# Attention's value products of a head for all 512 queries at once, with two heads of turned probabilities kept, in a three-part block kernel on Trainium2

## The chip, the cores and the metric

The kernel runs on one core of a Trainium2 chip. The metric is the device time of one execution in microseconds (us), here the median over several executions. TensorE (PE, with its weight loads shown apart as PEld), VectorE (DVE), ScalarE (ACT) and GpSimd (POOL) each run their own instruction stream in order and meet at semaphores. SyncE (SP) issues most of the transfers.

## The reference

A sequence of 512 tokens of width 1024 passes two layers of one kind (three mixers side by side and a mixture of experts) and then one layer of another kind with a dense feed-forward. The change touches the first two layers. There, an input projection gives, among others, a query part of rank 256 and a key/value part of rank 128 per token; both are normalised and multiplied by weights into 8 heads of queries, keys and values. What attention computes for a head is:

```python
s = (jnp.einsum('bqhd,bkhd->bhqk', qn_b, k_nope)
     + jnp.einsum('bqhr,bkr->bhqk', qr_b, k_rope)).astype(F32) * scale
p = jax.nn.softmax(s, axis=-1).astype(v.dtype)
return jnp.einsum('bhqk,bkhd->bqhd', p, v)
```

Two scans (an mLSTM and an SSD, each in both directions) follow from the same projection. Then comes the product with `w_out`, a layer norm and the experts.

## The kernel before

The program is a row of stages with a barrier of all engines between them. In each of the first two layers these are, among others, `in_projection`, `mla` (attention), `scans`, `norm_stage` (product with `w_out` and layer norm), a router and the experts. Numbers are kept at full precision by splitting a factor into a high and a low part (type fp32r): a product is three matmuls, `TERMS = ((0, 0), (0, 1), (1, 0))`. The high part is a cast by ACT, the low part a subtraction by DVE or POOL.

`mla` works in 32 tiles, i = 4h + t for the 8 heads h and the 4 blocks t of 128 queries, as a software pipeline written out by hand. The order of every engine's instructions is that of its loop over steps. In step s, PE (L555 to L570) does:

- `scores_of(s)` (L528): 3 matmuls of 512 columns into one of four banks, which must be free of the tile four before.
- `turned(s-3)` (L536): 4 transposes of the normalised probabilities into bank 4 or 5. It waits for the tile to be normalised and for the low part of tile s-5.
- `values_of(u, ks)` (L551) from step 6 on: for half a head u (256 queries) and two of the four key blocks, 6 matmuls of 256 columns with 64 columns of weights, into `O` (bank 6). A half head takes two steps. Its first step waits for the low parts of its two tiles; the first half of a head also waits for `head_home`, the copy of the previous head out of `O`.
- at t = 0 `query(h+1)` (L507), at t = 1 `key(h+1)` (L512), for h up to 6; in head 0 also `value(t)` (L517).

ACT in step s does: the copy of turned tile s-4 into `PT` as its high part (L595); at t = 2 from step 10 on, the copy of the finished head out of `O` (L599); at t = 1 the high part of the next query (L579), at t = 2 that of the next key (L585); the exponential of tile s (L609); and at t = 3 of heads 1 to 4 a cast of 512 columns for the scans (`KQ`, L616). DVE in step s does: the row maximum of tile s (L640), the reciprocal of the row sum of tile s-1 (L646), the low part of tile s-4 into `PT` (L653), the home copy of the next query at t = 0 (L626), the low part of the next key at t = 2 (L632). POOL normalises the tiles (L686) and makes the low part of the next query (L677).

`PT` is a ring of three half heads. `CQ` holds the normalised query and key/value inputs (three planes of 512 columns); it is written by `in_projection` in place (L429, L432) and read by `mla`. `raw` is a ring of four 1 MB weight chunks: `in_projection` reads its ten chunks of `w_in` through it, chunk i in slot i % 4, and `w_low` counts the chunks that POOL (L470) has finished with. In `mla`, slots 2 and 3 hold attention's weights, and SP loads the first two chunks of `w_out` into slots 0 and 1 (L498); `norm_stage` takes them (ACT, L1073, after `out_in` has reached 32). In `scans` SP issues 16 loads of gate rows `ROW` into a ring of 6 (L725); from s = 6 on each waits for the decay of stream s-6.

Of the kernel before, what the change touches and what calls it, by code (L numbers as in the profile page):

```python
# [21 lines left out]
F32 = mybir.dt.float32  # L22
F32R = mybir.dt.float32r
I32 = mybir.dt.int32
ALU = mybir.AluOpType
# [3 lines left out]
P = 128  # L29
S = 512  # L30
NT = S // P
# [14 lines left out]
C_QN, C_KVN, C_CW, C_CB, C_DS, C_SN, C_SGN, C_SB, C_AL, C_IB, C_MN, C_LG, C_LB, C_L2G, C_L2B, C_N = 0, 2, 3, 33, 39, 41, 43, 44, 45, 46, 47, 49, 57, 65, 73, 81  # L46
# [7 lines left out]
TERMS = ((0, 0), (0, 1), (1, 0))  # L54
# [157 lines left out]
def in_projection(nc, m, layer, mx, a, XS, WS):  # L212
# [11 lines left out]
    with stage(nc, "in_projection", *names) as (block, sems):  # L224
# [21 lines left out]
        def _(pe):  # L246
# [38 lines left out]
            for t in range(NT):  # L285
                if t == 2:
                    pe.wait_ge(m.mla_in, 16)
                    pe.wait_ge(home, K0 - 7)
                    pe.wait_ge(home, KV2 + 1)
                    pe.matmul(m.ps[K0 % 8][0:64, :], m.w_mla[:, 2048:2112], mx.CQ[:, 2, :], start=True, stop=True).then_inc(unit_done, 1)  # L290
                    pe.wait_ge(home, Q0 - 7)
                    pe.wait_ge(home, Q2 + 1)
                    for k in range(2):
                        last = pe.matmul(m.ps[Q0 % 8][:, :], m.w_mla[:, k * 1024:k * 1024 + P], mx.CQ[:, k, :], start=(k == 0), stop=(k == 1))
                    last.then_inc(unit_done, 1)
                pe.wait_ge(home, V[t] - 7)
                step = 0
                for k in range(KD):
                    for hw, hx in TERMS:
                        last = pe.matmul(m.ps[V[t] % 8][:, 0:256], XS[:, hx, k, t * P:(t + 1) * P], WS[:, i % 2, hw, k * 256:(k + 1) * 256],  # L300
                                         start=(step == 0), stop=(step == 3 * KD - 1))
                        step += 1
                last.then_inc(unit_done, 1)
# [59 lines left out]
        def _(dve):  # L363
# [62 lines left out]
            bank = home_of(GT)  # L426
            dve.tensor_copy(mx.GN[:, :, :, :].rearrange("p a t r -> p (a t r)"), bank[:, 0:2 * NT * GR]).then_inc(home, 1)
            dve.wait_ge(inv_rms, 1)
            dve.scalar_tensor_tensor(out=mx.CQ[:, 2, :], in0=mx.CQ[:, 2, :], scalar=m.CP[:, C_KVN:C_KVN + 1], in1=RS[0], op0=ALU.mult, op1=ALU.mult).then_inc(home, 1)  # L429
            dve.wait_ge(inv_rms, 2)  # L430
            for c in range(2):
                last = dve.scalar_tensor_tensor(out=mx.CQ[:, c, :], in0=mx.CQ[:, c, :], scalar=m.CP[:, C_QN + c:C_QN + c + 1],  # L432
                                                in1=RS[1], op0=ALU.mult, op1=ALU.mult)
            last.then_inc(home, 1)
            dve.wait_ge(kr_high, 1)
# [40 lines left out]
def mla(nc, m, layer, mx, a):  # L476
# [5 lines left out]
    with stage(nc, "mla", *names) as (block, sems):  # L482
# [10 lines left out]
        @block.sync  # L493
        def _(sp):
            sp.dma_start(m.gate_dram, mx.NM[0:GR, :]).then_inc(rows_out, 16)
            sp.wait_ge(rows_out, 16)
            for q in range(2):
                sp.dma_start(m.raw[:, q, :], m.d["w_out"][bass.ds(layer, 1), q].rearrange("a p n -> p (a n)")).then_inc(m.out_in, 16)  # L498

        @block.tensor  # L500
        def _(pe):

            def query(h):
                if h >= 2:
                    pe.wait_ge(k_low, h - 1)
                for k in range(2):
                    last = pe.matmul(Q[:, :], wq[:, k, h * P:(h + 1) * P], mx.CQ[:, k, :], start=(k == 0), stop=(k == 1))  # L507
                last.then_inc(q_done, 1)

            def key(h):  # L510
                pe.wait_ge(q_home, h)
                pe.matmul(Q[0:64, :], wk[:, h * 64:(h + 1) * 64], mx.CQ[:, 2, :], start=True, stop=True).then_inc(k_done, 1)  # L512

            def value(t):
                if t >= 1:
                    pe.wait_ge(v_low, t)
                pe.matmul(O[:, :], mx.CQ[:, 2, t * P:(t + 1) * P], wv, start=True, stop=True).then_inc(v_done, 1)  # L517

            def scores_of(i):
                h, t = divmod(i, NT)  # L520
# [15 lines left out]
                    last = pe.transpose(m.ps[4 + i % 2][:, k * P:(k + 1) * P], PR[:, i % 4, k * P:(k + 1) * P], m.ident[:, :])  # L536
                last.then_inc(probs_t, 1)

            def values_of(u, ks):

                h, half = divmod(u, 2)
                if ks[0] == 0:
                    pe.wait_ge(pt_low, 2 * u + 2)
                    if u == 0:
                        pe.wait_ge(v_low, NT)
                    if half == 0 and h >= 1:
                        pe.wait_ge(head_home, h)
                n = 0
                for k in ks:
                    for hv, hp in TERMS:  # L550
                        last = pe.matmul(O[0:64, half * 256:(half + 1) * 256], a.VS[:, hv, k, h * 64:(h + 1) * 64], a.PT[:, u % 3, hp, k, :],  # L551
                                         start=(k == 0 and n == 0), stop=(k == NT - 1 and n == 3 * len(ks) - 1))
                        n += 1
                last.then_inc(pv, 1)

            for step in range(NI + 6):
                h, t = divmod(step, NT)
                if step < NI:
                    scores_of(step)
                if 3 <= step < NI + 3:  # L560
                    turned(step - 3)
                if step >= 6:
                    u, part = divmod(step - 6, 2)
                    values_of(u, (2 * part, 2 * part + 1))
                if step < NI:
                    if t == 0 and h + 1 < HEADS:
                        query(h + 1)
                    if t == 1 and h + 1 < HEADS:
                        key(h + 1)
                    if h == 0:  # L570
                        value(t)

        @block.scalar
        def _(act):
# [9 lines left out]
                    act.wait_ge(scores, NT * (h - 1))  # L584
                act.copy(a.KS[h % 2][0:64, 0, :], Q[0:64, :]).then_inc(k_high, 1)  # L585

            for step in range(NI + 7):
                h, t = divmod(step, NT)
                if 4 <= step < NI + 4:
                    i = step - 4  # L590
                    act.wait_ge(probs_t, i + 1)
                    u = i // 2
                    if u >= 3:
                        act.wait_ge(pv, 2 * (u - 2))
                    act.copy(a.PT[:, u % 3, 0, :, i % 2 * P:(i % 2 + 1) * P], m.ps[4 + i % 2][:, :].rearrange("p (k n) -> p k n", k=NT)).then_inc(pt_high, 1)  # L595
                if step >= 10 and t == 2:
                    hp = (step - 10) // NT
                    act.wait_ge(pv, 4 * (hp + 1))
                    act.copy(m.XT[64 * (hp % 2):64 * (hp % 2) + 64, hp // 2, :], O[0:64, :]).then_inc(head_home, 1)  # L599
                if step < NI:  # L600
                    if h + 1 < HEADS:
# [18 lines left out]
        def _(dve):  # L620
# [13 lines left out]
            for step in range(NI + 4):  # L634
# [11 lines left out]
                    dve.reciprocal(a.RC[:, i % 4:i % 4 + 1], a.SM[:, i % 4:i % 4 + 1]).then_inc(inv_sum, 1)  # L646
                if step >= 4:
                    i = step - 4
                    u = i // 2
                    dve.wait_ge(pt_high, i + 1)  # L650
                    if u >= 3:
                        dve.wait_ge(pv, 2 * (u - 2))
                    dve.tensor_tensor(a.PT[:, u % 3, 1, :, i % 2 * P:(i % 2 + 1) * P], m.ps[4 + i % 2][:, :].rearrange("p (k n) -> p k n", k=NT),  # L653
                                      a.PT[:, u % 3, 0, :, i % 2 * P:(i % 2 + 1) * P].bitcast(F32), ALU.subtract).then_inc(pt_low, 1)
                if step < NI:
                    if h + 1 < HEADS:
                        if t == 0:
# [28 lines left out]
                pool.tensor_scalar(PR[:, i % 4, :], PR[:, i % 4, :], a.RC[:, i % 4:i % 4 + 1], None, ALU.mult).then_inc(probs_normed, 1)  # L686


def scans(nc, m, mx, g):

# [16 lines left out]
    with stage(nc, "scans", *names) as (block, sems):  # L709
# [10 lines left out]
        @block.sync  # L720
        def _(sp):
            for s in range(NS):
                if s >= RR:
                    sp.wait_ge(decay, 4 * (s - RR + 1))
                sp.dma_start(g.ROW[:, s % RR, :], m.gate_dram[row_of[s]:row_of[s] + 1, :].to_broadcast([P, S])).then_inc(row_in[s % RR], 16)  # L725

        @block.gpsimd
        def _(pool):
# [1916 lines left out]
def sb(nc, ctx, name, *shape):  # L2645

    return ctx.enter_context(nc.sbuf_tensor(f"{name}_{nc.next_id()}", list(shape), F32))


def sbr(nc, ctx, name, *shape):  # L2650

    return ctx.enter_context(nc.sbuf_tensor(f"{name}_{nc.next_id()}", list(shape), F32R))
# [7 lines left out]
def build(nc, d, out):  # L2660
    with ExitStack() as ctx:
# [24 lines left out]
        with ExitStack() as c1:  # L2686
# [14 lines left out]
            for layer in range(DEPTH):  # L2701
# [15 lines left out]
                with ExitStack() as c2:  # L2717
# [11 lines left out]
                    mx.GN = sb(nc, c2, "GN", P, 2, NT, GR)  # L2729
                    mx.XN = sb(nc, c2, "XN", P, NT, 256)  # L2730
                    with ExitStack() as c3:
                        mx.CQ = sb(nc, c3, "CQ", P, 3, S)
                        mx.KRT = sb(nc, c3, "KRT", P, S)
                        mx.TP = m.XT[:, 7, :]
                        a = Bag()
                        a.QS = [sbr(nc, c3, "QS", P, 2, S)]
                        a.KS = [sbr(nc, c3, "KS", P, 2, S)]
                        with ExitStack() as c4:
                            WS = sbr(nc, c4, "WS", P, 2, 2, KD * 256)
                            if layer == 0:  # L2740
                                transpose_stage(nc, m, XS0, first_loads, layer_params)
                            in_projection(nc, m, layer, mx, a, XS0, WS)
# [4 lines left out]
                        a.QS.append(sbr(nc, c3, "QS", P, 2, S))  # L2747
                        a.KS.append(sbr(nc, c3, "KS", P, 2, S))
                        a.VS = sbr(nc, c3, "VS", P, 2, NT, S)
                        a.PT = sbr(nc, c3, "PT", P, 3, 2, NT, 256)  # L2750
                        a.NM = sb(nc, c3, "NM", P, 4)
                        a.SM = sb(nc, c3, "SM", P, 4)
                        a.RC = sb(nc, c3, "RC", P, 4)
# [1 line left out]
                    with ExitStack() as c3:  # L2755
# [11 lines left out]
                        g.YI = c3.enter_context(nc.sbuf_tensor(f"YI_{nc.next_id()}", [P, 2, S], F32, side="right"))  # L2767
                        g.DEN = sb(nc, c3, "DEN", P, S)
                        g.RD = sb(nc, c3, "RD", P, S)
                        scans(nc, m, mx, g)  # L2770
                with ExitStack() as c2:
                    ln = Bag()
                    ln.GB = sb(nc, c2, "GB", P, 2 * D)
# [310 lines left out]
```

## Time and profile before

| | |
|---|---|
| median of three runs | 1982.55 us (1981.88 to 1986.97) |
| profiled execution, first to last instruction | 1984.4 us |
| mean granted TensorE clock over the span | 0.928 of full speed |
| PE busy over the span | 86% |
| `mla` of layer 0 | from 153.4 us to 241.5 us |
| `mla` of layer 1 | from 765.6 us to 853.8 us |

The page of the profile gives the span of the profiled execution; no other time of that same execution is listed. The busy shares of the whole span are means over stages with different limits, so what the change is worth has to be read from the two `mla` stages, which together take 176 of the 1984 us.

### The profile page before, as it was taken

Reading aid. Unit: us, or ns where it says so; the run is one execution under the profiler, and the core shown is the slowest. Engines: PE = TensorE matmul, PEld = TensorE weight load, DVE = VectorE, ACT = ScalarE, POOL = GpSimd, SP = SyncE. Lnnn points to the kernel's source line nnn. Section 1 sums busy time; section 2 is a strip of 40 time slices with the busy share of each in tenths; the row PEclk is TensorE's granted clock in tenths of the full one; section 3 lists DMA queues with packets and bytes.
Section 4 is the critical chain, followed back from the end, with each engine's and each line's share of the span. In section 5 each row is a group of like instructions: output and inputs, shape, how many; then the busy total and the mean of one; then the engine's idle time right before and its main releaser. Section 6 shows DMA issues by size and latency. Waiting matters only on the chain. (4 is left out here: it accounts for less than half of the span.)

```text
span 1984.4 us, 22134 instructions
## 1 busy us (share of the span) xinstructions
PE 1707.1 (86%) x8018; PEld 1330.5 (67%) x8018; DVE 1153.0 (58%) x1721; ACT 901.3 (45%) x1371; POOL 634.5 (32%) x337
## 2 busy tenths in 40 slices
PE   5999997849982999988949992699896689999998
PEld 4876743748871876752737872587686578888887
DVE  3936565559975745746858985487455424233242
ACT  3246576238875235756327883435443331111112
POOL 2336632112211434731201210153622124444442
PEclk9999998969995999989969996799898899999999
DMA  4201011069954211020257983320000223222221
GB/s 186 85 32 45 30 57 64 12 275 346 374 216 187 97 54 45 1 70 16 85 210 305 365 324 131 132 97 31 21 1 1 85 109 115 90 101 102 90 85 43
DMA packets 40480, 233.93 MB, mean 118 GB/s; under 512 B 9316, under 2 KB 9700, under 8 KB 20660
## 3 DMA queue, kind: packets, MB, share of 16 engines
q1 hardware_dynamic: 31012, 215.46, 28.6%
q0 software_dynamic: 9216, 16.80, 2.3%
q8 instruction: 65, 1.06, 0.2%
q14 instruction: 43, 0.35, 0.1%
q10 hardware_dynamic: 144, 0.26, 0.1%
HBM read 226.03 MB, written 23.23 MB: 126 GB/s over the span
## 5 line engine op out<-in xcount | busy, mean ns | idle before, releaser
L259 PE MATMUL bank<-XS,WS 128*128 128x512 f32 x864 | 207.4, 403 | 15.8 <-DVE WS L384 15.8
L2561 POOL TENSOR_TENSOR WS<-ring,WS 128x2048 fp32r<-128x2048 f32 x31 | 149.3, 4817 | 188.2 <-ACT WS L2543 188.2
L259 PEld LDWEIGHTS bank<-XS,WS 128*128 128x128 f32 x864 | 166.0, 192 | 56.9 <-DVE WS L384 16.4
L1382 PE MATMUL bank<-WS,XS 128*128 128x512 f32 x768 | 189.1, 403 | 1.1 <-DVE XS L1502 1.1
L2543 ACT CAST WS<-ring 128x2048 fp32r<-128x2048 f32 x31 | 59.3, 1913 | 271.4 <-PE bank L2578 143.8
L2578 PE MATMUL bank<-XS,WS 128*128 128x512 f32 x768 | 174.9, 389 | 2.7 <-DVEq L2616 2.7
L2596 PE MATMUL bank<-WS,US 128*128 128x512 f32 x768 | 174.7, 389 | 0.0
L1382 PEld LDWEIGHTS bank<-WS,XS 128*128 128x128 f32 x768 | 146.1, 194 | 32.2 <-DVE XS L1502 1.9
L2578 PEld LDWEIGHTS bank<-XS,WS 128*128 128x128 f32 x768 | 144.1, 188 | 32.7 <-POOLq L2557 2.9
L2596 PEld LDWEIGHTS bank<-WS,US 128*128 128x128 f32 x768 | 144.2, 188 | 29.9
L1846 PE MATMUL bank<-XS,WS 128*128 128x512 f32 x576 | 135.6, 396 | 3.6 <-POOLq L2035 2.6
L1846 PEld LDWEIGHTS bank<-XS,WS 128*128 128x128 f32 x576 | 109.1, 190 | 28.7 <-POOLq L2035 2.8
L470 POOL TENSOR_TENSOR WS<-raw,WS 128x2048 fp32r<-128x2048 f32 x18 | 83.9, 4659 | 114.5 <-ACT WS L314 114.5
L686 POOL TENSOR_SCALAR XT<-XT,RC 128x512 f32<-128x512 f32 x64 | 100.2, 1567 | 45.0 <-DVE RC L646 44.8
L1345 POOL DMA_INDIRECT mixed_rows<-YE,table x32 | 33.5, 1047 | 248.4 <-DVE table L1519 147.2
L2633 DVE TENSOR_TENSOR X<-X,bank 128x512 f32<-128x512 f32 x32 | 22.0, 688 | 141.6 <-PE bank L2596 141.6
L1406 PE MATMUL bank<-DS,HT 128*128 128x512 f32 x384 | 98.1, 405 | 6.2 <-DVE DS L1509 6.1
L1496 DVE TENSOR_TENSOR WS<-raw,WS 128x2048 fp32r<-128x2048 f32 x32 | 73.1, 2289 | 27.1 <-ACT WS L1443 27.1
L1406 PEld LDWEIGHTS bank<-DS,HT 128*128 128x128 f32 x384 | 72.4, 194 | 21.2 <-issue 6.5
L1006 PE MATMUL bank<-WS,XS 128*128 128x512 f32 x360 | 83.5, 392 | 0.0
L314 ACT CAST WS<-raw 128x2048 fp32r<-128x2048 f32 x18 | 34.3, 1906 | 103.5 <-PE bank L259 103.5
L2038 POOL TENSOR_TENSOR WS<-ring,WS 128x2048 fp32r<-128x2048 f32 x11 | 53.5, 4864 | 79.5 <-ACT WS L1868 79.5
(531 smaller groups left out, 3486.4 us busy)
## 6 DMA issues: line engine op xcount, KB each, us to landing
raw<-in_w_exp SPq DMA_DIRECT2D x16, 2048.0 KB, 14.8
DN<-in_w_exp SPq DMA_DIRECT2D x32, 1024.0 KB, 10.5
ring<-in_w_ff SPq DMA_DIRECT2D x32, 1024.0 KB, 4.8
raw<-in_w_in SPq DMA_DIRECT2D x20, 1024.0 KB, 4.8
GU<-in_w_exp SPq DMA_DIRECT2D x8, 2048.0 KB, 17.1
XT<-in_w_exp SPq DMA_DIRECT2D x8, 2048.0 KB, 17.5
ring<-in_w_in SPq DMA_DIRECT2D x12, 1024.0 KB, 5.1
raw<-in_w_out SPq DMA_DIRECT2D x8, 1024.0 KB, 4.8
```

The lines of the kernel that those rows point to most:

```text
L259: last = pe.matmul(m.ps[g % 8][:, :], WS[:, i % 2, hw, at:at + P], XS[:, hx, k, :], start=(step == 0), stop=(step == 3 * KD - 1))
L470: pool.tensor_tensor(WS[:, i % 2, 1, :], m.raw[:, i % 4, :], WS[:, i % 2, 0, :].bitcast(F32), ALU.subtract).then_inc(w_low, 1)
L686: pool.tensor_scalar(PR[:, i % 4, :], PR[:, i % 4, :], a.RC[:, i % 4:i % 4 + 1], None, ALU.mult).then_inc(probs_normed, 1)
L1006: last = pe.matmul(m.ps[2 * t + half][:, :], XS[:, hx, 4 * kh + k, t * P:(t + 1) * P], WS[:, 2 * kh + half, hw, k * S:(k + 1) * S], start= ...
L1382: last = pe.matmul(m.ps[2 + e % 2][:, :], r.XS[:, e % 2, hx, 4 * half + k, :], r.WS[:, half, hw, k * S:(k + 1) * S], start=(half == 0 and ...
L1406: last = pe.matmul(m.ps[5 + half][:, :], r.HT[:, hx, f * P:(f + 1) * P], r.DS[:, hw, at:at + S], start=(n == 0), stop=(n == 5))
L1496: dve.tensor_tensor(r.WS[:, half, 1, :], r.GU[e % 4][:, half * 4 * S:(half + 1) * 4 * S], r.WS[:, half, 0, :].bitcast(F32), ALU.subtract). ...
L1846: last = pe.matmul(bank[u][:, :], q.WS[:, i % 2, hw, at:at + P], b.XS[:, hx, k, :], start=(step == 0), stop=(step == 3 * KD - 1))
L2543: act.copy(f.WS[:, q % 2, 0, :], f.ring[:, q % 4, :]).then_inc(w_high, 1)
L2561: pool.tensor_tensor(f.WS[:, q % 2, 1, :], f.ring[:, q % 4, :], f.WS[:, q % 2, 0, :].bitcast(F32), ALU.subtract).then_inc(w_low, 1)
L2578: last = pe.matmul(m.ps[mine + u % 4][:, :], f.WS[:, q % 2, hw, k * 256 + c * P:k * 256 + (c + 1) * P], f.XS[:, hx, k, :], start=(n == 0), ...
L2596: last = pe.matmul(bank[:, :], f.US[:, hx, 4 * kh + k, t * P:(t + 1) * P], f.WS[:, q % 2, hw, k * S:(k + 1) * S], start=(kh == 0 and n == ...
```

## The change

The value products of a head are made in four steps of three matmuls, each over all 512 queries and one block of keys, in place of two halves with two steps of six matmuls over 256 queries. They start at step 8 in place of step 6, and the loop has two steps more. `PT` keeps two whole heads in place of three half heads. The copy of a finished head by ACT moves from t = 2 (from step 10) to t = 0 (from step 12). To make room, the normalised inputs move from `CQ` into slot 0 of `raw` under the name `CN`, so `in_projection` waits for `w_low` at 9 before it writes them; `CQ` and `KRT` are freed after `in_projection`. The two loads of `w_out` move from `mla` into `scans`, behind the row loads s = 7 and s = 9.

```diff
@@ in_projection
             dve.wait_ge(inv_rms, 1)
+            dve.wait_ge(w_low, NB - 1)
-            dve.scalar_tensor_tensor(out=mx.CQ[:, 2, :], in0=mx.CQ[:, 2, :], scalar=m.CP[:, C_KVN:C_KVN + 1], in1=RS[0], op0=ALU.mult, op1=ALU.mult).then_inc(home, 1)
+            dve.scalar_tensor_tensor(out=mx.CN[:, 2, :], in0=mx.CQ[:, 2, :], scalar=m.CP[:, C_KVN:C_KVN + 1], in1=RS[0], op0=ALU.mult, op1=ALU.mult).then_inc(home, 1)
...
@@ mla, SP
             sp.wait_ge(rows_out, 16)
-            for q in range(2):
-                sp.dma_start(m.raw[:, q, :], m.d["w_out"][bass.ds(layer, 1), q].rearrange("a p n -> p (a n)")).then_inc(m.out_in, 16)
@@ mla, PE
-            def values_of(u, ks):
-
-                h, half = divmod(u, 2)
-                if ks[0] == 0:
-                    pe.wait_ge(pt_low, 2 * u + 2)
-                    if u == 0:
+            def values_of(h, k):
+
+                if k == 0:
+                    pe.wait_ge(pt_low, NT * (h + 1))
+                    if h == 0:
                         pe.wait_ge(v_low, NT)
-                    if half == 0 and h >= 1:
+                    if h:
                         pe.wait_ge(head_home, h)
-                n = 0
-                for k in ks:
-                    for hv, hp in TERMS:
-                        last = pe.matmul(O[0:64, half * 256:(half + 1) * 256], a.VS[:, hv, k, h * 64:(h + 1) * 64], a.PT[:, u % 3, hp, k, :],
-                                         start=(k == 0 and n == 0), stop=(k == NT - 1 and n == 3 * len(ks) - 1))
-                        n += 1
+                for n, (hv, hp) in enumerate(TERMS):
+                    last = pe.matmul(O[0:64, :], a.VS[:, hv, k, h * 64:(h + 1) * 64], a.PT[:, h % 2, hp, k, :],
+                                     start=(k == 0 and n == 0), stop=(k == NT - 1 and n == 2))
                 last.then_inc(pv, 1)
 
-            for step in range(NI + 6):
+            for step in range(NI + 8):
...
-                if step >= 6:
-                    u, part = divmod(step - 6, 2)
-                    values_of(u, (2 * part, 2 * part + 1))
+                if step >= 8:
+                    values_of(*divmod(step - 8, NT))
@@ mla, ACT
-            for step in range(NI + 7):
+            for step in range(NI + 9):
...
-                    u = i // 2
-                    if u >= 3:
-                        act.wait_ge(pv, 2 * (u - 2))
-                    act.copy(a.PT[:, u % 3, 0, :, i % 2 * P:(i % 2 + 1) * P], m.ps[4 + i % 2][:, :].rearrange("p (k n) -> p k n", k=NT)).then_inc(pt_high, 1)
-                if step >= 10 and t == 2:
-                    hp = (step - 10) // NT
-                    act.wait_ge(pv, 4 * (hp + 1))
+                    hi, ti = divmod(i, NT)
+                    if hi >= 2:
+                        act.wait_ge(pv, NT * (hi - 1))
+                    act.copy(a.PT[:, hi % 2, 0, :, ti * P:(ti + 1) * P], m.ps[4 + i % 2][:, :].rearrange("p (k n) -> p k n", k=NT)).then_inc(pt_high, 1)
+                if step >= 12 and t == 0:
+                    hp = (step - 12) // NT
+                    act.wait_ge(pv, NT * (hp + 1))
                     act.copy(m.XT[64 * (hp % 2):64 * (hp % 2) + 64, hp // 2, :], O[0:64, :]).then_inc(head_home, 1)
@@ mla, DVE: the same ring of two heads and the same wait for pv in the low part
...
@@ scans, SP
                 sp.dma_start(g.ROW[:, s % RR, :], m.gate_dram[row_of[s]:row_of[s] + 1, :].to_broadcast([P, S])).then_inc(row_in[s % RR], 16)
+                if s in (RR + 1, RR + 3):
+                    q = (s - RR) // 2
+                    sp.dma_start(m.raw[:, q, :], m.d["w_out"][bass.ds(layer, 1), q].rearrange("a p n -> p (a n)")).then_inc(m.out_in, 16)
@@ build
-                        mx.CQ = sb(nc, c3, "CQ", P, 3, S)
-                        mx.KRT = sb(nc, c3, "KRT", P, S)
+                        mx.CN = m.raw[:, 0, 0:3 * S].rearrange("p (c n) -> p c n", c=3)
...
-                        a.PT = sbr(nc, c3, "PT", P, 3, 2, NT, 256)
+                        a.PT = sbr(nc, c3, "PT", P, 2, 2, NT, S)
```

## Rows read from the trace of the kernel before

**Rows 1.** Windows: the two mla stages, busy us per engine, clock, DMA.
```profile
153.30:241.50 88.20, 84.28 (x466) 61.17 (x466) 57.60 (x118) 58.00 (x127) 59.82 (x40) 1.00 0.07 26
765.50:853.70 88.20, 84.29 (x466) 61.20 (x466) 57.61 (x118) 58.02 (x127) 59.83 (x40) 1.00 0.07 26
```

**Rows 2.** Waits in mla of layer 0: us in total, times, longest.
```profile
PE bank L551 <- ACT XT L599: 0.5, 1, 0.5
```

**Rows 3.** Timeline around 193 us: weight loads of one step at t = 3.
```profile
192.10 0.54 PEld L528 LDWEIGHTS bank<-KS,QS 128*128 128x128 f32 x3
...
192.74 0.54 PEld L536 LDWEIGHTS bank<-ident,XT 128*128 128x128 f32 x4
...
193.25 0.71 PEld L551 LDWEIGHTS bank<-PT,VS 128*64 128x64 f32 x6
...
193.94 0.53 PEld L528 LDWEIGHTS bank<-KS,QS 128*128 128x128 f32 x3
```

**Rows 4.** Timeline 222 to 256 us: heads 6 and 7 and the tail.
```profile
225.33 0.57 ACT L595 CAST PT<-bank 128x512 fp32r<-128x512 f32 x1
...
225.88 0.71 PEld L551 LDWEIGHTS bank<-PT,VS 128*64 128x64 f32 x6
...
228.99 0.58 ACT L595 CAST PT<-bank 128x512 fp32r<-128x512 f32 x1
...
229.59 0.58 ACT L599 COPY XT<-bank 64x512 f32<-64x512 f32 x1
...
230.28 0.67 PEld L551 LDWEIGHTS bank<-PT,VS 128*64 128x64 f32 x6 [0.70 <-issue]
...
230.93 0.55 PEld L528 LDWEIGHTS bank<-KS,QS 128*128 128x128 f32 x3
...
233.35 0.57 ACT L595 CAST PT<-bank 128x512 fp32r<-128x512 f32 x1
...
235.97 0.42 PEld L536 LDWEIGHTS bank<-ident,XT 128*128 128x128 f32 x4
...
236.85 2.83 PEld L551 LDWEIGHTS bank<-PT,VS 128*64 128x64 f32 x24 [0.46 <-DVE PT L653]
...
237.28 0.69 DVE L653 TENSOR_TENSOR PT<-bank,PT 128x512 fp32r<-128x512 f32 x1 [0.51 <-ACT PT L595]
239.98 0.58 ACT L599 COPY XT<-bank 64x512 f32<-64x512 f32 x1 [2.73 <-PE bank L551]
```

**Rows 5.** Timeline 168 to 190 us: step 12, behind a KQ cast.
```profile
184.26 0.61 ACT L616 CAST KQ<-MQ 128x512 fp32r<-128x512 f32 x1
...
184.77 0.58 ACT L595 CAST PT<-bank 128x512 fp32r<-128x512 f32 x1
184.82 0.71 PEld L551 LDWEIGHTS bank<-PT,VS 128*64 128x64 f32 x6
```

**Rows 6.** The same timeline: scores at t = 2 of head 1 and 2.
```profile
169.73 0.53 PEld L528 LDWEIGHTS bank<-KS,QS 128*128 128x128 f32 x3 [0.81 <-issue]
...
180.01 0.53 PEld L528 LDWEIGHTS bank<-KS,QS 128*128 128x128 f32 x3 [0.81 <-ACT XT L609]
```

**Rows 7.** The same timeline: step 8, low part of tile 3, turn of tile 5.
```profile
173.27 0.66 DVE L653 TENSOR_TENSOR PT<-bank,PT 128x512 fp32r<-128x512 f32 x1
...
174.05 0.53 PEld L536 LDWEIGHTS bank<-ident,XT 128*128 128x128 f32 x4
```

**Rows 8.** DMA issues 150 to 300 us: KB each, median us to landing.
```profile
raw<-in_w_out SPq DMA_DIRECT2D x2, 1024.0 KB, 5.8
```

**Rows 9.** Timelines of SP and ACT: row load s = 7, first use of w_out.
```profile
254.81 0.32 SPq L725 DMA_DIRECT2D ROW<-gate_rows  x1
...
330.75 1.05 ACT L1073 CAST WS<-raw 128x1024 fp32r<-128x1024 f32 x1 [1.92 <-PEq L77]
```

**Rows 10.** Timeline 130 to 430 us: end of the input projection.
```profile
138.30 0.75 DVE L429 SCALAR_TENSOR_TENSOR CQ<-CQ,CP,XT 128x512 f32<-128x512 f32 x1 [5.14 <-ACT XT L350]
...
147.55 1.31 POOL L472 TENSOR_TENSOR QS<-XT,QS 128x512 fp32r<-128x512 f32 x1 [20.09 <-ACT QS L359]
```

More of the change, by code:

```diff
@@ L289, in _ @@
                     pe.wait_ge(home, KV2 + 1)
-                    pe.matmul(m.ps[K0 % 8][0:64, :], m.w_mla[:, 2048:2112], mx.CQ[:, 2, :], start=True, stop=True).then_inc(unit_done, 1)
+                    pe.matmul(m.ps[K0 % 8][0:64, :], m.w_mla[:, 2048:2112], mx.CN[:, 2, :], start=True, stop=True).then_inc(unit_done, 1)
                     pe.wait_ge(home, Q0 - 7)
@@ L293, in _ @@
                     for k in range(2):
-                        last = pe.matmul(m.ps[Q0 % 8][:, :], m.w_mla[:, k * 1024:k * 1024 + P], mx.CQ[:, k, :], start=(k == 0), stop=(k == 1))
+                        last = pe.matmul(m.ps[Q0 % 8][:, :], m.w_mla[:, k * 1024:k * 1024 + P], mx.CN[:, k, :], start=(k == 0), stop=(k == 1))
                     last.then_inc(unit_done, 1)
@@ L428, in _ @@
             dve.wait_ge(inv_rms, 1)
-            dve.scalar_tensor_tensor(out=mx.CQ[:, 2, :], in0=mx.CQ[:, 2, :], scalar=m.CP[:, C_KVN:C_KVN + 1], in1=RS[0], op0=ALU.mult, op1=ALU.mult).then_inc(home, 1)
+            dve.wait_ge(w_low, NB - 1)
+            dve.scalar_tensor_tensor(out=mx.CN[:, 2, :], in0=mx.CQ[:, 2, :], scalar=m.CP[:, C_KVN:C_KVN + 1], in1=RS[0], op0=ALU.mult, op1=ALU.mult).then_inc(home, 1)
             dve.wait_ge(inv_rms, 2)
             for c in range(2):
-                last = dve.scalar_tensor_tensor(out=mx.CQ[:, c, :], in0=mx.CQ[:, c, :], scalar=m.CP[:, C_QN + c:C_QN + c + 1],
+                last = dve.scalar_tensor_tensor(out=mx.CN[:, c, :], in0=mx.CQ[:, c, :], scalar=m.CP[:, C_QN + c:C_QN + c + 1],
                                                 in1=RS[1], op0=ALU.mult, op1=ALU.mult)
@@ L506, in query @@
                 for k in range(2):
-                    last = pe.matmul(Q[:, :], wq[:, k, h * P:(h + 1) * P], mx.CQ[:, k, :], start=(k == 0), stop=(k == 1))
+                    last = pe.matmul(Q[:, :], wq[:, k, h * P:(h + 1) * P], mx.CN[:, k, :], start=(k == 0), stop=(k == 1))
                 last.then_inc(q_done, 1)
@@ L511, in key @@
                 pe.wait_ge(q_home, h)
-                pe.matmul(Q[0:64, :], wk[:, h * 64:(h + 1) * 64], mx.CQ[:, 2, :], start=True, stop=True).then_inc(k_done, 1)
+                pe.matmul(Q[0:64, :], wk[:, h * 64:(h + 1) * 64], mx.CN[:, 2, :], start=True, stop=True).then_inc(k_done, 1)
             def value(t):
@@ L516, in value @@
                     pe.wait_ge(v_low, t)
-                pe.matmul(O[:, :], mx.CQ[:, 2, t * P:(t + 1) * P], wv, start=True, stop=True).then_inc(v_done, 1)
+                pe.matmul(O[:, :], mx.CN[:, 2, t * P:(t + 1) * P], wv, start=True, stop=True).then_inc(v_done, 1)
             def scores_of(i):
@@ L648, in _ @@
                     i = step - 4
-                    u = i // 2
+                    hi, ti = divmod(i, NT)
                     dve.wait_ge(pt_high, i + 1)
[L651 to L654, printed above, removed]
+                    if hi >= 2:
+                        dve.wait_ge(pv, NT * (hi - 1))
+                    dve.tensor_tensor(a.PT[:, hi % 2, 1, :, ti * P:(ti + 1) * P], m.ps[4 + i % 2][:, :].rearrange("p (k n) -> p k n", k=NT),
+                                      a.PT[:, hi % 2, 0, :, ti * P:(ti + 1) * P].bitcast(F32), ALU.subtract).then_inc(pt_low, 1)
                 if step < NI:
@@ L686, in _, with scans @@
                 pool.tensor_scalar(PR[:, i % 4, :], PR[:, i % 4, :], a.RC[:, i % 4:i % 4 + 1], None, ALU.mult).then_inc(probs_normed, 1)
-def scans(nc, m, mx, g):
+def scans(nc, m, layer, mx, g):
     streams = [("mlstm", h, d, h) for h in range(4) for d in range(2)]
@@ L2738, in build @@
                         with ExitStack() as c4:
+                            mx.CQ = sb(nc, c4, "CQ", P, 3, S)
+                            mx.KRT = sb(nc, c4, "KRT", P, S)
                             WS = sbr(nc, c4, "WS", P, 2, 2, KD * 256)
@@ L2769, in build @@
                         g.RD = sb(nc, c3, "RD", P, S)
-                        scans(nc, m, mx, g)
+                        scans(nc, m, layer, mx, g)
                 with ExitStack() as c2:
```

## The prediction

> **What bounds the kernel now.** I read the windows of the two `mla` stages first. Each lasts 88.2 us, PE is busy for 84.3 of them at a granted clock of 1.00 (2.4 GHz), no other engine for more than 60, and both layers are alike to 0.02 us [rows 1]. So each term below is worked out in layer 0 and taken twice. Then the timeline. In a step without query or key, PE's weight loads stand back to back: scores start at 192.10, the turn at 192.74, the value products at 193.25, the next scores at 193.94 [rows 3]. That is 0.64 + 0.51 + 0.69 = 1.84 us with no gap: PE sets the pace, and the other engines run one to three steps beside it.
>
> The waits of PE on the copy of a finished head were the third view. Of eight such copies in a layer just one kept PE waiting [rows 2]. It is the one of step 30, in head 7, where no key product stands between the last products of a head and the first of the next. There ACT's order decides. It copies turned tile 26 at 228.99, then the head at 229.59, and the products start at 230.28 [rows 4]. Two steps earlier, with no copy due, the tile copy starts at 225.33 and the products at 225.88 [rows 4]. The products thus start 1.29 after the tile copy in place of 0.55: the copy of a head costs PE 0.74 us where nothing covers it. At t = 2 of the other heads PE has about 1 us of key products ahead of that place, and they cover it.
>
> **The change part by part.**
>
> *Half as many value products, twice as wide.* 192 of 256 columns become 96 of 512 in each layer; the columns streamed are the same. Six narrow ones take 0.69 us; three of 512 columns, by the scores in the same rows, 0.64 [rows 3]. The gain is 0.05 us a step; its lower bound is nothing (the same columns), its upper bound this 0.05, since no row shows a 512-column product in a shorter slot. I take 0.05. From step 8 to step 31 it counts in 24 steps, but in the five where PE then waits for ACT (next part) it only lengthens the wait: 19 x 0.05 = 0.95 us a layer.
>
> The Trainium skill, "TensorE: Matmul & The Clock Gate", section "Back-to-back issue gap", gives N/2.4 + 2.5 ns a product, an estimate of 6 x 109.2 against 3 x 215.8 ns, so a gain of 0.008 us a step. The trace shows six times that. By the page's rule the sum below would be 1.6 us higher, 12.8 in place of 11.2.
>
> *The head copy moves from t = 2 to t = 0.* Now the last products of a head close step t = 3, which has neither query nor key, and the next head's products come after only scores and turn, as in step 30. ACT can't be earlier: after the exponential of the step before, it first copies the turned tile. Queued behind PE's wait stand the query, the next scores, and with them every engine. Steps 12, 16, 20, 24 and 28 have it. In 24 and 28 it costs the 0.74 worked out above. In 12, 16 and 20 ACT's `KQ` cast (0.61) comes ahead of the tile copy too: there the tile copy starts at 184.77 and the products at 184.82 [rows 5]. With 1.29 after the tile copy they start at 186.06, a wait of 1.24. Sum: 3 x 1.24 + 2 x 0.74 = 5.20 us. The wait of step 30 goes: -0.74. Lower bound of this part nothing, if PE has hidden slack to make it up (rival 2); upper bound 5.20. I take 4.46 net, since PE shows no slack.
>
> *Steps 6 and 7 lose their products.* That is 2 x 0.69 = 1.38 us less for PE early on. But step 8 can't start its turn before the low part of tile 3, which ends at 173.27 + 0.66 = 173.93; PE turns at 174.05 today [rows 7]. What is late next is thus DVE's chain. I take nothing; the upper bound is 1.38 us a layer.
>
> *The tail.* I count from T, the start of the last scores (230.93 now). Today the last turn is at T + 5.04, the last half head's low part ends at T + 7.04, and ACT takes the last head at T + 9.05 [rows 4]. In the new order ACT copies tile 28 at T + 2.42 as now, and head 5 behind it, so the products of step 32 start at T + 3.71 and take 0.64. The turn of tile 30 and its products follow until T + 5.49. The turn of tile 31 (0.51) and the last two product steps of head 6 end at T + 7.27. Now the copy of head 6 stands alone between two heads. ACT started 0.32 us after the end of 24 product slots of 0.117 [rows 4], so it copies at T + 7.59, and PE resumes 0.69 later at T + 8.28. Low part 31, about two us behind its turn as now, is earlier. All 12 products of head 7 follow: 12 x 0.213 = 2.56. ACT takes the last head at T + 11.16, 2.1 us later than now. Lower bound: just the 2.56 against today's 1.38 of the last half, 1.2 us.
>
> *The rest I cost at nothing.* The new wait for `w_low` in `in_projection`: POOL had been idle for 20 us at 147.55, so it was done by 127.5, and DVE gets there at 138.3 [rows 10]. Without that cover DVE would stand still until POOL has finished chunk 8. Writing to `raw` in place of `CQ` keeps sizes and instructions. The ring of two heads makes ACT and DVE wait at step 4h + 4 for products that closed the step before. The head copy waits for the same event, so this is already counted. The two `w_out` loads stand on SP's queue behind the row load s = 7 (254.81) and two further on. 1 MB lands in 5.8 us, and `norm_stage` first reads it at 330.75 [rows 8, 9]: some 60 us of cover. A row load behind one is late by 5.8 us at most, and it is issued six streams ahead in a stage whose streams take over 4 us each. In `mla` nothing queued behind these loads.
>
> **Sum.** Per layer 4.46 - 0.95 + 2.1 = 5.6 us, for both 11.2. The profiled span is 1984.4; what lies around it is not shown, and the median of the runs, 1982.55, is 1.85 below the span, so I add the difference to the median: 1993.8 us, slower by 0.57%. I count changes within 0.3% (6 us) as no change: about what a measurement of this kernel can tell.
>
> **Rivals.**
> 1. *The start is kept.* If step 8 is not held by DVE, the 1.38 us a layer are a gain: 1993.8 - 2.8 = 1991.0. Rows 7 speak against it, by 0.12 us.
> 2. *The other side: the copy is paid for where it left.* At t = 2 the scores of head 2 start after 0.81 us that the profile puts down to ACT [rows 6], and ACT no longer copies a head in that step. If this idle time is ACT's, each of five heads gets back up to 0.81: 4.05 a layer, and 1993.8 - 8.1 = 1985.7, no change. It decides if the 0.81 falls below about 0.3. Against it: head 1, with no copy due, has the same 0.81 [rows 6], so it looks like the drain behind the key product.
> 3. *A row load is late.* If `w_out` holds up a row that the scans need, 5.8 us twice a layer at most: up to 2017. The six-stream lead speaks against it.
> 4. *The change brings what its count says.* If narrow products cost PE more than their slots show and the three wide ones free more than 0.05, the gain must exceed 5.6 us in 24 steps of a layer, 0.23 a step, to break even. The slot of 0.213 for a wide product leaves no room.
>
> **Chances.** Forecast 0.62 (its own range 1990 to 1998), rival 1 0.15, rival 2 0.13, rival 3 0.03, rival 4 0.04, the rest 0.03. With forecast, 1 and 3, less a few hundredths for spread between runs, slower is 0.80. Rival 2 and that spread make no change 0.16, and faster is 0.04. Range: the bounds together give per layer, at the low end, 4.46 - 1.2 + 1.2 - 1.38 = 3.1, which is 1988.7, and at the high end 4.46 + 2.1 = 6.6, which is 1995.7. Down to 1986 takes in most of rival 2. Runs of before differ by 5 us, so the top is 1998.
>
> **What would show it.** 96 value matmuls a layer, in threes, with 0.64 to the next scores. At steps 12, 16 and 20 PE waits some 1.2 us for L599's copy at its new line, at 24 and 28 some 0.7, at 30 not at all. `mla` takes about 93.8 us in place of 88.2, and its last head copy comes 11 us after the last scores. The turn of step 8 starts as now. The scans take the same time, with no wait for a row. Wrong would be: `mla` no longer than 90 us, the 0.81 at t = 2 gone, or a difference of over 2 us outside the two stages.

## The result and the profile after

The changed kernel takes 1992.15 us in the median of five runs (1987.21 to 1995.61), the kernel before 1981.88 in five (1980.48 to 1986.97): a ratio of 1.005 with a 95% interval of 1.0033 to 1.0066. That is 10.3 us slower; forecast were 11.2 us, as 1993.8 us in a range of 1986 to 1998.

The windows of the two attention stages after answer to [rows 1] (columns as there: length, busy us of PE, PEld, DVE, ACT and POOL, clock, DMA share, GB/s):

```profile
152.50:246.50 94.00, 85.02 (x370) 52.02 (x370) 57.64 (x118) 58.01 (x127) 59.72 (x40) 1.00 0.01 2
...
766.80:860.90 94.10, 85.10 (x370) 52.03 (x370) 57.63 (x118) 57.99 (x127) 59.72 (x40) 1.00 0.01 2
```

Each stage has 96 matmuls fewer (370 for 466) and is longer by 5.9 us (94.06 and 94.10 from its first transfer to the scans' first, for 88.16 and 88.17). The two make 11.8 us, more than the whole difference of the medians. PE is busy 0.8 us longer in a stage 5.9 us longer: it waits. The view of waits in the stage of layer 0 says for whom (left of the arrow who waited, right of it for whom; us in total, times, longest). Before, PE's waits for the head copy were one of 0.5 [rows 2]:

```profile
ACT XT L593 <- PE bank L547: 3.9, 2, 3.1
PEld bank L547 <- issue: 3.6, 4, 1.1
PE bank L547 <- ACT XT L593: 3.5, 5, 0.9
```

L547 are the value products, L593 is ACT's copy of a finished head. Of the five hand-overs the view puts four to the copy and that of step 16 to a low part by DVE that ends at the same moment; the products of that step need low parts that were done 1.9 us before, so there too it is the copy. Step 12 in the timeline answers to [rows 5], step 24 to the stretch of [rows 4] that showed the one wait of before:

```profile
183.23 0.61 ACT L610 CAST KQ<-MQ 128x512 fp32r<-128x512 f32 x1
...
183.74 0.58 ACT L589 CAST PT<-bank 128x512 fp32r<-128x512 f32 x1
184.22 0.58 ACT L593 COPY XT<-bank 64x512 f32<-64x512 f32 x1
...
184.91 0.42 PEld L547 LDWEIGHTS bank<-PT,VS 128*64 128x64 f32 x3 [1.13 <-issue]
184.94 0.87 PE L547 MATMUL bank<-PT,VS 128*64 128x512 f32 x3 [0.92 <-ACT XT L593]
```
```profile
217.31 0.58 ACT L589 CAST PT<-bank 128x512 fp32r<-128x512 f32 x1
...
217.91 0.58 ACT L593 COPY XT<-bank 64x512 f32<-64x512 f32 x1
...
218.60 0.42 PEld L547 LDWEIGHTS bank<-PT,VS 128*64 128x64 f32 x3 [0.73 <-issue]
```

Cast, tile copy, head copy follow one another on ACT without a gap, and PE's weight loads stand still for 1.13 us where the cast is ahead and 0.73 where it isn't. The tail of layer 0, from the last scores on, is the third place:

```profile
233.57 0.65 PEld L527 LDWEIGHTS bank<-KS,QS 128*128 128x128 f32 x3
...
241.27 0.58 ACT L593 COPY XT<-bank 64x512 f32<-64x512 f32 x1 [0.80 <-PE bank L547]
...
241.96 2.49 PEld L547 LDWEIGHTS bank<-PT,VS 128*64 128x64 f32 x12 [1.22 <-DVE PT L647]
241.99 2.95 PE L547 MATMUL bank<-PT,VS 128*64 128x512 f32 x12 [0.76 <-ACT XT L593]
244.97 0.58 ACT L593 COPY XT<-bank 64x512 f32<-64x512 f32 x1 [3.13 <-PE bank L547]
```

The last head copy starts 11.40 us after the last scores (244.97 - 233.57), against 9.05 before [rows 4]. All 12 products of head 7 stand behind the copy of head 6.

The profiled execution of after has a span of just 1985.5 us, 1.1 more than that of before, though its attention stages alone are 11.8 us longer. It is the fastest of its five runs (1987.21). The stage of router and experts, which the change doesn't touch, takes 202.7 and 204.2 us in it, and 206.1 twice in the profile of before; over all profiles of this study it lies between 202.3 and 206.1. In this pair of profiles the two make up half of the 10.7 us by which all that lies outside attention is shorter; the other half is spread over the other stages. Attention stages agree between their two layers to 0.1 us. So below the stage's length decides, and the medians follow it only roughly.

### The profile page after: what moved, and what is told of

It is laid out like the page before. It is cut to its first block and busy times, and to the rows that moved or that the text cites. A ratio compares the mean times of both kernels' runs of the same rounds, so it can differ in the third digit from the quotient of the medians.

```text
span 1985.5 us, 21746 instructions
## 1 busy us (share of the span) xinstructions
PE 1701.4 (86%) x7826; PEld 1308.6 (66%) x7826; DVE 1150.5 (58%) x1721; ACT 899.9 (45%) x1371; POOL 634.1 (32%) x337
```

## The experiments

The starts of the scores in the weight-load timeline give the length of each PE step. The table has the steps that differ (us, layer 0; step 10 stands for all steps at t = 2 from there on, which agree to 0.03; the stage runs from its first transfer to the first one of the scans, "last scores at" counts from its start, and "rest" is what follows the start of the last scores):

| | before | after | e1 two out banks | e2 copy first | e3 narrow | e5 cast moved | e7 before, two banks |
|---|---|---|---|---|---|---|---|
| step 6 | 1.83 | 1.14 | 1.13 | 1.13 | 1.14 | 1.13 | 1.83 |
| step 8 | 3.25 | 3.79 | 3.80 | 3.80 | 3.81 | 3.80 | 3.24 |
| step 10 | 1.83 | 1.71 | 1.69 | 1.72 | 1.83 | 1.69 | 1.83 |
| step 12 | 3.23 | 4.44 | 3.34 | 3.95 | 4.32 | 3.91 | 3.24 |
| step 16 | 3.24 | 4.57 | 3.33 | 4.06 | 4.43 | 4.06 | 3.24 |
| step 20 | 3.23 | 4.44 | 3.35 | 3.95 | 4.32 | 3.91 | 3.24 |
| step 24 | 3.23 | 4.05 | 3.35 | 3.58 | 3.91 | 4.03 | 3.23 |
| step 28 | 1.84 | 2.39 | 1.82 | 1.93 | 2.37 | 2.40 | 1.84 |
| step 30 | 2.52 | 1.83 | 1.83 | 1.83 | 1.84 | 1.82 | 1.84 |
| last scores at | 77.54 | 81.08 | 76.50 | 78.71 | 81.34 | 79.57 | 76.88 |
| rest | 10.62 | 12.98 | 11.79 | 13.18 | 12.93 | 13.02 | 10.29 |
| stage | 88.16 | 94.06 | 88.29 | 91.89 | 94.27 | 92.59 | 87.17 |

**e1: the wait taken away.** The products of even and odd heads go to two banks (bank 3 comes from the scores, which keep three), so a head's products wait only for the copy of the head before the last. Theory: the wait for the copy and the tail are the loss. Rival: the longer pipeline, the moved inputs or the late loads are, and the waits only show it.

```diff
+        OB = (m.ps[6], m.ps[3])
...
-                    if h:
-                        pe.wait_ge(head_home, h)
+                    if h >= 2:
+                        pe.wait_ge(head_home, h - 1)
...
-                    last = pe.matmul(O[0:64, :], a.VS
+                    last = pe.matmul(OB[h % 2][0:64, :], a.VS
...
-                    last = pe.matmul(m.ps[i % 4][:, :], a.QS
+                    last = pe.matmul(m.ps[i % 3][:, :], a.QS
```

> The changed kernel with the products of even and odd heads in two banks, so that a head's products wait for the copy of the head before the last (the scores get three banks in place of four). Theory (the wait of PE for ACT's copy of a head, plus the longer tail, is the loss): all five waits at steps 12 to 28 and the two in the tail go; per layer 24 x 0.05 = 1.2 us and the 0.74 of step 30 are gained against the kernel before, and a tail of about 0.9 us is lost, so the attention stage takes about 87.1 us (94.1 changed, 88.2 before) and the kernel about 1980 us. Rival (the longer pipeline, the moved inputs or the late loads cost the time, the waits only show it): the stage stays above 92 us.

1981.06 us, against 1981.44 for the kernel before, measured beside it: a ratio of 0.9998 (0.9988 to 1.0007). The stage takes 88.29 us. At step 12 the products now start while the tile copy is still running, and ACT takes the finished head later, with nobody waiting:

```profile
184.90 0.59 ACT L590 CAST PT<-bank 128x512 fp32r<-128x512 f32 x1
184.92 0.47 PEld L548 LDWEIGHTS bank<-PT,VS 128*64 128x64 f32 x3
...
185.37 0.58 ACT L594 COPY XT<-bank 64x512 f32<-64x512 f32 x1
```

This kernel has every other part of the change: the wide products, the two-head ring, the inputs in `raw`, the late loads. The theory holds, and the rival falls. But the stage was expected at 87.1, and the 1.2 us that are missing have to be found (they are added up under "Sum" below).

**e2: the order on ACT.** The head copy (the block with L593) stands ahead of the tile copy in the same step; nothing else differs.

```diff
+                if step >= 12 and t == 0:
+                    ... head copy
                 if 4 <= step < NI + 4:
                     ... tile copy
-                if step >= 12 and t == 0:
-                    ... head copy
```

> The changed kernel with ACT's copy of a finished head ahead of the copy of the turned tile in the same step. Theory (PE waits because the copy stands behind the tile copy in ACT's order): each of five waits gets shorter by the 0.58 us of a tile copy, so about 2.8 us per layer, the stage takes about 91.3 us in place of 94.1, the kernel about 1986.5. Rival (PE waits for the latency between the products' end and the copy, not for the order): the stage stays at 94.

1991.2 us, ratio 1.005 (1.0033 to 1.0067); by the median no better than after, by the stage 2.2 us a layer (91.89 and 91.94). The five steps shrink by 0.49, 0.51, 0.49, 0.47 and 0.46 us; the tail grows by 0.2, since the low parts there now come behind. Order is the cause, but a tile copy costs the queue about 0.48 us, not 0.58. ACT begins the next instruction that early (183.74 to 184.22 in step 12 above).

**e5: the cast.** The KQ cast moves from t = 3 of heads 1 to 4 to t = 0 of the next head, behind the exponential.

```diff
-                    if t == 3 and 1 <= h <= 4:
-                        c, kq = divmod(h - 1, 2)
+                    if t == 0 and 2 <= h <= 5:
+                        c, kq = divmod(h - 2, 2)
```

> The changed kernel with ACT's KQ cast moved from t = 3 of heads 1 to 4 to t = 0 of the next head, behind the exponential, so that it no longer stands ahead of the head copy. Theory: steps 12, 16 and 20 fall from 4.44, 4.57 and 4.44 us to the 4.05 of step 24, where no cast stands ahead: 1.3 us per layer, stage 92.8 us, kernel about 1989.5. Rival (PE catches the cast up elsewhere, or waits for latency alone): stage 94.1.

1988.15 us, ratio 1.0035 (1.0022 to 1.0048), stage 92.59 and 92.63. Steps 12, 16 and 20 fall to 3.91, 4.06 and 3.91, that is to about step 24's length (4.03), and steps 24 and 28 stay: the cast is on PE's path in three heads of a layer.

**e3: narrow products in the new order.** Each wide product is two of 256 columns again.

```diff
-                for n, (hv, hp) in enumerate(TERMS):
-                    last = pe.matmul(O[0:64, :], ... a.PT[:, h % 2, hp, k, :],
+                for half in range(2):
+                    at = slice(half * 256, (half + 1) * 256)
+                    for n, (hv, hp) in enumerate(TERMS):
+                        last = pe.matmul(O[0:64, at], ... a.PT[:, h % 2, hp, k, at],
```

> The changed kernel with the order kept, but each value product again as two of 256 columns, six in a step. Theory: a step costs 0.05 us more, in the 19 steps without a wait, and the last 12 products become 24 (0.25 us): 1.2 us more per layer, stage 95.3 us, kernel about 1994.5. Rival by the rule of 2.5 ns per product: 0.008 a step, stage 94.3.

1992.78 us, ratio 1.0057 (1.0041 to 1.0074); the stage takes 94.27 and 94.26, 0.2 us more than with wide products. The 0.05 us a step of the theory is too high by some four times. Half as many matmuls over the same columns save PE next to nothing here.

**e4: the loads alone.** The kernel before with the two loads of `w_out` in the scans.

```diff
-            for q in range(2):
-                sp.dma_start(m.raw[:, q, :], ...).then_inc(m.out_in, 16)
...
+                if s in (RR + 1, RR + 3):
+                    q = (s - RR) // 2
+                    sp.dma_start(m.raw[:, q, :], ...).then_inc(m.out_in, 16)
```

> The kernel before with just the two loads of w_out moved into the scans. Theory: hidden, no change (1982 us within 2; the scans stage 89.2 us as before, no wait for a row). Rival (a row load stands behind 1 MB): the scans longer by up to 5.8 us per load and layer.

1980.36 us, ratio 0.9998 (0.9988 to 1.0009). The scans take 89.9 and 88.8 us, before 89.2 and 89.3; in all kernels with the loads there they take 88.5 to 90.0. In layer 0 POOL waits for a row just once, for the first one, which is issued ahead of both loads. Hidden, as expected.

**e6: the tail.** e1 with the products of head 7 by halves of 256 queries, so that the first half needn't wait for the last low part.

```diff
+            def last_values(part):
+                h = HEADS - 1
+                at = slice(part * 256, (part + 1) * 256)
+                pe.wait_ge(pt_low, NT * h + 2 * part + 2)
...
-                if step >= 8:
+                if 8 <= step < NI + 4:
                     values_of(*divmod(step - 8, NT))
+                if NI + 4 <= step < NI + 6:
+                    last_values(step - NI - 4)
```

> The kernel with two out banks (88.29 us a stage, last scores at 76.50 and 11.79 us from there to the end) with the last head's products by halves of 256 queries, as in the kernel before, so that the first half runs under the last turns. Theory (in the tail 12 wide products stand behind the last low part where 12 narrow ones stood): the tail falls to the 10.6 us of the kernel before, stage 87.1 us, kernel 1979 us against 1981.4. Rival (the tail is longer because products of head 6 stand in it, two steps late): it stays near 11.8, stage 88.3.

1982.34 us, ratio 1.0005 (0.9996 to 1.0013); stage 87.95 and 87.94, rest 11.51. The theory of the tail falls, with 0.28 of the 1.2 us it asked for, and its rival holds for the rest. Weight loads from the last turn on, in e6:

```profile
235.47 0.42 PEld L536 LDWEIGHTS bank<-ident,XT 128*128 128x128 f32 x4 [0.34 <-POOL XT L695]
235.85 1.17 PEld L548 LDWEIGHTS bank<-PT,VS 128*64 128x64 f32 x6
237.12 2.87 PEld L560 LDWEIGHTS bank<-PT,VS 128*64 128x64 f32 x24
```

Behind the last turn stand six wide products of head 6 and then all of head 7, with no wait for a low part (e1 had one of 0.50 us there). PE is simply at work. The two steps by which all value products moved back are paid here; steps 6 and 7, which they left, gave 0.13 us.

**e7: the kernel before with two out banks.** The bank edit of e1 in the old order.

> The kernel before with two out banks for even and odd heads and three for the scores, nothing else. Theory: the one wait it had, step 30, falls from 2.52 to 1.83 us; stage 87.5 us in place of 88.17, kernel about 1980. Rival (three banks for the scores bring a wait of their own): stage 88.2 or more.

1980.85 us, ratio 0.9993 (0.9984 to 1.0002), stage 87.17 and 87.18. Step 30 falls to 1.84 and the tail by 0.33, where the products of head 7 had waited for the copy of head 6. So before, two of the eight copies kept PE waiting and not just one, as I had read from [rows 2]: the profile puts the wait in the tail to DVE [rows 4, at 236.85]. It has the shortest stage of all these kernels, 1.0 us below before, but two layers of that are not told from no change by the medians.

## Why the prediction was right, step by step

*What sets the pace.* PE, confirmed: nearly every us that PE waited in steps 12 to 28 is in the stage's length. Between e1 and after, which differ in the out banks, those steps differ by 4.70 us and the last scores by 4.58 (76.50 to 81.08).

*The head copy at t = 0.* The mechanism was right and the size a little high. Steps 12 to 28 cost 1.10 + 1.24 + 1.09 + 0.70 + 0.57 = 4.70 us against e1, where I had 5.20. I had taken the price of every hand-over from step 30, and the copy there is that of head 5. In all these kernels but e2, which has another order, the copy of an even head (rows 0 to 63 of `XT`) starts 0.46 to 0.48 us after the tile copy ahead of it, that of an odd head (rows 64 to 127) 0.59 to 0.61, wherever it follows without a wait. Heads 0 and 1 in the kernel before:

```profile
179.38 0.58 ACT L595 CAST PT<-bank 128x512 fp32r<-128x512 f32 x1
179.84 0.58 ACT L599 COPY XT<-bank 64x512 f32<-64x512 f32 x1
...
189.65 0.58 ACT L595 CAST PT<-bank 128x512 fp32r<-128x512 f32 x1
...
190.25 0.58 ACT L599 COPY XT<-bank 64x512 f32<-64x512 f32 x1
```

Steps 12, 20 and 28 hand over even heads and cost less than the 1.24 and 0.74 forecast; steps 16 and 24 hand over odd ones and cost 1.24 and 0.70. That the rows of `XT` are the reason is not tested. The wait of step 30 went about as forecast (0.74; 0.66 by e7's last scores).

*Half as many value products: the step that failed in size.* I had 0.05 us a step, 0.95 a layer. e1 against e7, both without waits for a copy, gives 76.88 - 76.50 = 0.38 by the last scores; 0.11 of it comes from steps 6 to 8, so the products save 0.27. e3 says the same, 0.26. I had read the spacing of weight loads as the slots of the products, and the weight loads run ahead by different amounts. In after, the load of the next scores follows that of the wide products by 0.57 us, less than the 0.64 forecast, but the load of the turn then comes another 0.79 behind, where it was 0.64 before [rows 3]:

```profile
181.93 0.48 PEld L547 LDWEIGHTS bank<-PT,VS 128*64 128x64 f32 x3
182.50 0.64 PEld L527 LDWEIGHTS bank<-KS,QS 128*128 128x128 f32 x3
183.29 0.49 PEld L535 LDWEIGHTS bank<-ident,XT 128*128 128x128 f32 x4
```

The matmuls themselves show nearly equal slots at t = 3, 0.78 us from six narrow products to the next scores in before (first two rows) and 0.78 from three wide ones in e1 (last two):

```profile
172.73 0.94 PE L551 MATMUL bank<-PT,VS 128*64 128x256 f32 x6
...
173.51 0.87 PE L528 MATMUL bank<-KS,QS 128*128 128x512 f32 x3
...
183.12 0.95 PE L548 MATMUL bank<-PT,VS 128*64 128x512 f32 x3
...
183.90 0.85 PE L528 MATMUL bank<-KS,QS 128*128 128x512 f32 x3
```

So steps at t = 2 look 0.14 us shorter by their weight loads (1.69 in e1 for 1.83 in e7, step 10), and steps at t = 0 take 0.1 of it back (3.34 for 3.24). The count of 96 and the stream of columns were right. The rule of the Trainium skill that I had set against my rows ("TensorE: Matmul & The Clock Gate", section "Back-to-back issue gap", where the page gives it for an isolated product; 0.008 us a step is an estimate from it) is nearer to these runs than the 0.05 that I called the trace's: they give 0.012 (0.27 us over the 22 steps from 9 to 30).

*Steps 6 and 7.* Nearly as forecast: they were put at nothing and gave 0.13 us. Step 6 is 0.69 shorter, step 7 no shorter at all (1.86 for 1.84), and step 8 takes 0.54 back. The turns of steps 7 and 8 wait for DVE's low parts; that of step 8:

```profile
172.37 0.66 DVE L647 TENSOR_TENSOR PT<-bank,PT 128x512 fp32r<-128x512 f32 x1
...
173.18 0.63 PE L535 MATMUL bank<-ident,XT 128*128 128x128 f32 x4 [0.38 <-DVE PT L647]
```

Its weight load starts 20.66 us into the stage (at 173.15), as it did before [rows 7]. Rival 1 is out.

*The tail.* 2.36 us for my 2.1. Of these 1.50 come with wide and late products (rest 11.79 in e1, 10.29 in e7), 1.19 with the waits for copies (12.98 in after, 11.79 in e1), and 0.33 of a wait that before had are gone. e6 splits the 1.50: 0.28 for products that can't be started by halves, the rest for those of head 6 that come two steps later.

*Sum.* By the last scores: 4.58 for the hand-overs, 0.66 less for the wait of step 30 and 0.38 less for the products and the start give 3.54. With 2.36 behind them it is 5.90 a layer, for 5.6 forecast. That the last scores came out so near the 3.51 forecast is luck: a gain and a wait were both put too high and cancelled. My range had a flaw: its low end keeps the hand-overs at 4.46, although I had put their lower bound at nothing. The 1.2 us that e1 lacked are the same errors: 0.8 of the products' gain (0.38 for 1.2), 0.3 in the tail (1.17 for 0.9) and 0.1 in step 30 (0.66 for 0.74).

*Rival 2* had put its hope in the 0.81 us ahead of the scores at t = 2. ACT copies no head there any more, and the row is the same:

```profile
178.97 0.53 PEld L527 LDWEIGHTS bank<-KS,QS 128*128 128x128 f32 x3 [0.81 <-ACT XT L603]
```

So this idle time isn't the copy's. That it is a drain behind the key product is argued, not shown. *Rival 3* falls with e4. In after the loads landed in 6.8 us (median, for 5.8 in attention) and nobody waited. *Rival 4* falls with e3.

*A sign of being wrong that appeared.* I had named a difference of over 2 us outside the two stages. In the profile of after it is there, 3.5 us in the experts of layer 0. But that stage, the same in every kernel here, lies anywhere from 202.3 to 206.1 in their profiles, and its two layers differ by 2.6 in e4 alone (202.6 and 205.2). So the sign was badly chosen and says nothing about the change.

## What to carry to other kernels

Halving the count of matmuls at the same number of columns bought almost nothing where PE streams them back to back (0.27 us of a stage of 88); ask first what it does to the places where one engine hands a bank to another. A hand-over that was covered by unrelated work (here a key product) loses its cover when the order shifts by two steps, and its price is the queue ahead of the copy on the other engine. A second bank took it away altogether here (4.6 us a layer). Products moved back in a pipeline are paid in its tail (1.2 us here), and the start gives back only what no other engine holds up there (0.1 us here, with DVE's low parts in the way). Read a slot from the length of whole steps or from the starts of the matmuls, not from the spacing of weight loads.

## What the runs showed of the hardware that was not expected

At the start of the scans of layer 0 the granted clock differs. Before, with PE idle for some 1.6 us between the last products and the first ones of the scans, it was 0.50 (1.2 GHz) from 244 to 248 us. After, the same work runs at 1.00 (2.4 GHz) in the first 4 us of the stage, and falls only later (columns as in the windows above):

```profile
246.50:250.50 4.00, 3.02 (x12) 2.14 (x12) 0.48 (x1) 0.00 (x0) 0.00 (x0) 1.00 0.50 144
250.50:254.50 4.00, 1.00 (x1) 0.50 (x2) 1.71 (x4) 2.69 (x9) 3.98 (x4) 0.87 0.72 254
254.50:258.50 4.00, 4.00 (x13) 2.40 (x11) 1.50 (x4) 1.56 (x6) 2.62 (x3) 0.70 0.19 66
```

The gap ahead was the same length (1.65 us), so what tells the two apart stays open. It is not shown to come of the change: e5, which runs the same instructions as after at this place, has 0.77 in the first 4 us of the scans and 0.50 in the next 4. The scans of after took 89.08 us all the same (89.19 before): behind their first products PE waits 3.9 us again, for DVE and ACT, and these for POOL's mask of the first row, which starts when that row has landed.

A tile copy by ACT (128x512, from a bank) lasts 0.58 us by its row, but the copy of an even head behind it starts 0.46 to 0.48 us after it, before that time is over. The copy of an odd head, whose rows go from 0 to 63 of the bank to 64 to 127 of `XT`, starts 0.59 to 0.61 after it, in both layers. No run tells whether the shift of rows is the cause.
